# Hybrid retention / gated DeltaNet trunk: the DeltaNet steps' solve, spread and levels one slot later, with a new first step, start and end

## The reference

```python
h = rmsnorm(x, norm_g)
proj = h @ w_in                      # 1024 -> 9232: rq rk rv rz | dq dk dv dz | beta, a | two gates
o_r = retention(rope(rq), rope(rk), rv)        # 4 heads, dk 128, dv 256, chunks of 128
o_r = groupnorm(o_r) * silu(rz)
dq, dk, dv = silu(causal_conv(dq, dk, dv))     # 4 taps
o_d = gated_deltanet(l2norm(dq), l2norm(dk), dv, beta, g)   # 8 heads of 128
o_d = o_d * rsqrt(mean(o_d**2) + EPS) * dn_g * silu(dz)
y = sigmoid(gr) * (o_r @ w_up_r) + sigmoid(gd) * (o_d @ w_up_d)
x = x + y @ w_o
```

```python
v_new = u_n - w_n @ state
o = q_n @ state + attn_n @ v_new
state = state * exp(gl) + k_n.T @ v_new
```

## Time and profile before

| | us |
|---|---|
| median of 3 runs | 2670.03 (2669.53 to 2670.82) |
| the profiled execution | 2671.89 |
| its span | 2670.1 |
| TensorE busy in it | 2640.1 (99%) |
| VectorE busy | 1730.1 (65%) |
| ScalarE busy | 679.9 (25%) |
| GpSimd busy | 832.2 (31%) |
| mean granted TensorE clock | 0.998 |

### The profile page before, as it was taken

The page is one execution under the profiler, slowest core; times in us unless marked ns, Lnnn a source line. Parts: engine busy times, 40 slices in busy tenths (PEclk is TensorE's granted clock), DMA queues, the critical chain, the costliest instruction groups (busy, mean ns, idle before and its releaser), DMA issues.

```text
span 2670.1 us, 39962 instructions
## 1 busy us (share of the span) xinstructions
PE 2640.1 (99%) x14850; PEld 2255.1 (84%) x14850; DVE 1730.1 (65%) x3864; ACT 679.9 (25%) x1370; POOL 832.2 (31%) x459
## 2 busy tenths in 40 slices
PE   8999999999999999999999999999999999999998
PEld 6788888888898899888878888888888998888887
DVE  7878777877756555434587778777777555553333
ACT  5233333333312222200142232323332221231001
POOL 3233333333312112435432323232323122232443
PEclk9999999999999999999999999999999999999999
DMA  4331222222211112434532222222222111133344
GB/s 171 96 88 53 74 74 76 65 73 76 71 52 46 40 35 74 127 96 122 163 93 84 76 70 68 69 84 65 71 70 73 50 50 42 40 105 100 98 138 146
DMA packets 292980, 217.76 MB, mean 82 GB/s; under 512 B 31698, under 2 KB 246052, under 8 KB 292532
## 3 DMA queue, kind: packets, MB, share of 16 engines
q1 hardware_dynamic: 254884, 151.20, 19.8%
q10 hardware_dynamic: 37904, 64.01, 7.1%
HBM read 176.30 MB, written 38.86 MB: 81 GB/s over the span
## 4 chain that ended last, share of the span: by engine, by line
PE 89%; DVE 4%; DMA 3%; issue 1%; POOL 1%; SPq 1%; ACT 1%; ACTq 0%; DVEq 0%
PE dense_ps L819 22%; PE dense_ps L823 22%; PE dense_ps L821 22%; PE work L802 3%; PE dense_ps L843 2%; PE dense_ps L844 2%; PE dense_ps L845 2%; PE work L1077 1%; DMA arena<-l_scratch 1%; PE work L1114 1%; PE work L1053 1%; PE work L1036 1%; PE work L1134 1%; PE work L1103 1%; PE work L1127 1%
## 5 line engine op out<-in xcount | busy, mean ns | idle before, releaser
L819 PE MATMUL dense_ps<-act_hi,w_hi 128*128 128x512 f32 x2560 | 1052.3, 411 | 2.5 <-DVE act_lo L1766 1.5
L823 PE MATMUL dense_ps<-act_hi,w_lo 128*128 128x512 f32 x2560 | 1002.8, 392 | 0.0
L821 PE MATMUL dense_ps<-act_lo,w_hi 128*128 128x512 f32 x2560 | 1000.5, 391 | 0.0
L2459 POOL TENSOR_TENSOR w_lo<-w_raw,w_hi 128x1024 fp32r<-128x1024 f32 x162 | 400.1, 2469 | 1014.8 <-ACT w_hi L1350 572.2
L823 PEld LDWEIGHTS dense_ps<-act_hi,w_lo 128*128 128x128 f32 x2560 | 480.7, 188 | 107.0
L819 PEld LDWEIGHTS dense_ps<-act_hi,w_hi 128*128 128x128 f32 x2560 | 482.9, 189 | 86.7 <-issue 3.0
L821 PEld LDWEIGHTS dense_ps<-act_lo,w_hi 128*128 128x128 f32 x2560 | 483.4, 189 | 79.6 <-issue 0.5
L1883 DVE SCALAR_TENSOR_TENSOR arena<-arena,cols 128x512 f32<-128x512 f32 x288 | 242.6, 842 | 5.1
L1350 ACT ACTIVATE w_hi<-w_raw 128x1024 fp32r<-128x1024 f32 x88 | 92.7, 1054 | 327.5 <-PE dense_ps L823 309.9
L1340 ACT ACTIVATE arena<-dense_ps 128x512 f32<-128x512 f32 x96 | 57.4, 598 | 264.6 <-PE dense_ps L823 264.6
L1897 DVE SCALAR_TENSOR_TENSOR arena<-arena 128x512 f32<-128x512 f32 x96 | 112.5, 1172 | 13.9 <-ACT arena L1356 13.9
(11 more groups left out here) (248 smaller groups left out, 4040.2 us busy)
## 6 DMA issues: line engine op xcount, KB each, us to landing
w_raw<-in_w_in SPq DMA_DIRECT2D x138, 512.0 KB, 3.9
gate_scratch<-arena ACTq DMA_DIRECT2D x64, 256.0 KB, 2.1
arena<-gate_scratch ACTq DMA_DIRECT2D x64, 256.0 KB, 2.8
arena<-l_scratch SPq DMA_DIRECT2D x62, 256.0 KB
w_raw<-in_w_out SPq DMA_DIRECT2D x18, 512.0 KB, 3.6
o_scratch<-arena ACTq DMA_DIRECT2D x32, 256.0 KB, 2.0
w_raw<-in_w_up_dn SPq DMA_DIRECT2D x16, 512.0 KB, 3.7
arena<-o_scratch ACTq DMA_DIRECT2D x32, 256.0 KB, 3.8
```

Of the source, the lines that this page charges most:

```text
L819: eng.matmul(dense_ps[:, to, :], w_hi[:, slot, k, :], hi[:, k, seg], start=(k == 0), stop=False)
L821: eng.matmul(dense_ps[:, to, :], w_hi[:, slot, k, :], lo[:, k, seg], start=False, stop=False)
L823: mm = eng.matmul(dense_ps[:, to, :], w_lo[:, slot, k, :], hi[:, k, seg], start=False, stop=(k == KT - 1))
L2459: eng.tensor_tensor(w_lo[:, slot, :, :], w_from[second][:, :, :], w_hi[:, slot, :, :].bitcast(F32), ALU.subtract)\
```

## The change

In the regular steps (`even`, `odd`, `even_last`) the solve begins at slot 4 instead of 3, the spread stands at slot 9 instead of 8, each level one slot later, and `vt` at 20; no tap is placed in slots 4 to 8 instead of 3 to 7, so that slot 3 takes one. The list of slot 9 already holds `ks` of chunk 3, and the spread comes behind it; `turn 0` and `level_v 0` come ahead of `xu` in slot 10. The splits of weights stay where they are.

The first step gets a list of its own: solve from slot 16, spread at 21, levels at 23 to 31, the masks on VectorE instead of GpSimd, splits of the high parts on ScalarE, low parts on VectorE as steps of their own (`low`), both halves of the `l_scratch` load on SyncE's queue. At the start, tile 6's transposes go ahead of the dense pieces, `norm_rows(0, 1)` comes one piece later, `norm_diag(0, 1)` behind the loop of norms, and the split of the first weight ahead of a silu. At the end the last output block is computed in two halves of 256 tokens (`last_pieces`), transposes and squares are regrouped accordingly, means and powers come earlier, and tiles 4 to 7 are stored in halves of 512 columns.

```diff
@@ unit_schedule, first step
-        at(6, "mask", 0)
-        at(8, "dec", 0)
+        at(8, "split", 1)
+        at(9, "mask", 0)
+        at(9, "dec", 0)
         at(10, "nl", 0)
+        at(10, "low", 1)
...
-        at(15, "qe")
-        at(16, "kq")
-        slots[15].insert(0, ("mask", 1))
-        at(19, "dec", 1)
-        solve, spread_at, vt = 17, 24, 34
+        at(17, "kq")
+        at(20, "split", 2)
+        at(21, "spread")
+        at(21, "turn", 0)
+        at(22, "low", 2)
+        at(23, "level_v", 0)
+        at(23, "mask", 1)
+        at(23, "qe")
+        at(25, "level_x", 0)
+        at(25, "kq_decay")
+        at(25, "mask_t", 1)
+        at(26, "turn", 1)
+        at(26, "level_v", 1)
...
+        solve, spread_at, vt = 16, 21, 33
@@ unit_schedule, regular steps
-        solve, spread_at, vt = 3, 8, 19
+        solve, spread_at, vt = 4, 9, 20
+    else:
+        solve, spread_at = 4, 9
     if kind != "odd_last":
         for k in range(BASE - 1):
             at(solve + k // 3, "solve", k)
-        at(spread_at, "spread")
-        for n in range(NLV):
-            if first or n:
+        for n in range(NLV if not first else 0):
+            if n == 0:
+                at(spread_at, "spread")
+            if n:
                 at(spread_at + 1 + 3 * n, "turn", n)
                 at(spread_at + 1 + 3 * n, "level_v", n)
                 at(spread_at + 3 + 3 * n, "level_x", n)
...
-            spread(0 if 3 <= n < 8 else 1 if n < 18 and n not in (12, 16) else 2)
+            spread(0 if solve <= n < spread_at else 1 if n < 18 and n not in (12, 16) else 2)
@@ SyncE, load of l_scratch
-                    for c in range(0, CPH if u else 2, 2):
+                    for c in range(0, CPH, 2):
@@ TensorE, start
             turn_in(CPH + 1)
+            turn_in(CPH + 2)
...
-                        if k == 0:
-                            turn_in(CPH + 2)
-                        if k == 2:
+                        if k == 1:
                             turn_in(CPH + 3)
...
-                        if k == CPH:
+                        if k == CPH + 1:
                             norm_rows(l, 1)
@@ VectorE, layer start
-                silu(l * DH, 0)
                 eng.wait_ge(dense_ok[0].sem, dense_ok[0].after(n + 1, 2))
                 split_w(n + BLK_FIRST, BLK_FIRST % 2, held=False)
+                silu(l * DH, 0)
@@ TensorE, the last output block, in halves of 256 tokens
+            def last_pieces():
+                g = n + BLK_OUT + NHALF * KT - 1
+                for part in range(2):
+                    to = 1 - part
+                    seg = slice(HALF + part * HALF // 2, HALF + (part + 1) * HALF // 2)
+                    dst = dense_ps[:, to, 0:HALF // 2]
...
@@ SyncE, stores
-            for i in range(CPH + 1):
+            for i in range(CPH):
                 eng.wait_ge(out_ok, 2 * i + 2)
                 store(i, slice(0, D_MODEL))
+            eng.wait_ge(out_ok, 9)
+            store(4, left)
+            eng.wait_ge(out_ok, 10)
+            store(4, right)
```

More of the change, by code:

```diff
@@ L228, in unit_schedule @@
                 break
-            if pieces % (2 * KT) == 0 and (pieces or kind not in ("first", "odd_last")):
+            if pieces % (2 * KT) == 0 and not first and (pieces or kind != "odd_last"):
                 step = ("split", pieces // (2 * KT))
[L231 to L234, removed]
+                waiting.insert(0, step)
                 if kind == "even_last" and step[1] == 2:
@@ L1246, in _ @@
                           ready=(lambda b, k: None if b else (ol_ok.sem, ol_ok.after(l, k + 1))) if j == 0 else None)
-                for i in range(NHALF * KT):
+                for i in range(NHALF * KT if more else NHALF * KT - 1):
                     b, j = i // KT, i % KT
@@ L1271, in _ @@
                         turn_out(3)
-            for i in range(CPH, NCH):
-                turn_late(i)
+            for part, k in last_pieces():
+                if part == 0 and k == 4:
+                    for tile in (4, 5):
+                        turn_next(tile)
+                if part and k == 3:
+                    for tile in (4, 5):
+                        turn_late(tile)
+                if part and k == 4:
+                    for c in range(4):
+                        mm = turn_chunk(7, 0, c)
+                    mm.then_inc(out_ps, 1)
+                    turn_next(6)
+            for tile in (6, 7):
+                turn_late(tile)
         @block.scalar
@@ L1472, in delta_unit @@
                                 ret_v(l * RH, gg, int(of[2]), half)
-                        elif what == "split" and kind in ("even", "odd"):
+                        elif what == "split" and (kind in ("even", "odd") or kind == "first" and step[1]):
                             idx = g0 + step[1] + 1
@@ L2104, in delta_unit @@
                                .then_inc(qe_s.sem, 1)
-                        elif what == "kq":
+                        elif what == ("kq_decay" if kind == "first" else "kq"):
                             eng.wait_ge(kq_ps.sem, kq_ps.after(tn, 1))
@@ L2419, in _ @@
                     eng.sem_inc(dense_free[i % 2].sem, 1)
-                    if i >= NHALF * KT - 2:
+                    if more and i >= NHALF * KT - 2:
                         eng.sem_inc(dense_ok[i % 2].sem, KT)
@@ L2432, in _ @@
                                 norm_lo(l + 1, 0, k - 1)
-                    if not more and i in (KT + 2, KT + 5):
-                        final_mean((i - KT - 2) // 3)
+                    if not more and i == KT + 2:
+                        final_mean(0)
                     if not more and i in (KT + 3, KT + 4):
@@ L2533, in delta_unit @@
                                 split_w(g + idx, idx % 2)
-                        elif what == "mask":
+                        elif what == "mask" and kind != "first":
                             w = tn + step[1]
@@ L2616, in _ @@
                         norm_lo(l + 1, 0, 2 * (i - KT - 3))
-                    if not more and i in (KT + 2, KT + 5):
-                        final_power((i - KT - 2) // 3)
+                    if not more and i in (KT + 2, KT + 4):
+                        final_power((i - KT - 2) // 2)
                 if more:
```

140 lines of the change are left out of this document (92 added, 48 removed).

## The result

| | before | after |
|---|---|---|
| median, us | 2670.43 (2669.53 to 2670.97, 4 runs) | 2717.55 (2715.15 to 2719.93, 4 runs) |
| profiled execution, its span | 2671.89, 2670.1 | 2718.55, 2716.7 |
| granted TensorE clock, mean | 0.998 | 0.998 |

The changed kernel is slower: the ratio is 1.0176, with a 95% interval of 1.016 to 1.0191, or 47.1 us by the medians. The forecast was 2709 us, 39 us slower, with a range of 2662 to 2735.

A forecast was written before the change was run, and what follows sets the result against it. TensorE was taken to bound the kernel. Spread hold +43.2 and even steps' turn +5.3, less 9.5 won (loads, first steps, start, end), gave +39.0 on 2670.0: 2709 us, range 2662 to 2735.

The forecast's parts named there:

- What bounds the kernel: Whole kernel: TensorE, busy 2640.1 of 2670.1 us, so any delay to it in a repeated step is paid in full.
- The spread under GpSimd's subtraction, +43.2: Regular steps: spread held until GpSimd's subtraction ends, `level_v0` 1.44 us late in each of 30 steps, +43.2 us.
- The even steps' turn, +5.3: Even steps: `level_x1` waits 0.38 us for the level 1 copy, now behind other VectorE work, 14 times, +5.3 us.
- The late loads of `l_scratch`, -2.4: Regular steps: late `l_scratch` loads no longer matter with the solve a slot later, -2.4 us.
- First steps, -3.9: First steps of the layers: 60% of 6.5 us of TensorE waits won, -3.9 us.
- Start -1.3, end -1.9: Start: transposes fill a wait and `norm_rows` comes later, -1.3 us; end: stores begin earlier, -1.9 us.
- B: Regular steps: the spread isn't held by GpSimd, only the other terms stay, 2666 us; chance 0.14.
- C: Regular steps: the solve's last instruction is caught by GpSimd too, `level_v0` waits 2.95 us, 2754 us; chance 0.10.
- D: Regular steps: spread and GpSimd share and slow each other, spread takes 1.38 us, 2679 us; chance 0.05.
- E: TensorE's clock falls with the new idle times, coming on top, inside the range's upper end; chance 0.03.

The follow-up runs named there:

- e3: Changed kernel, with GpSimd's subtraction for split 1 of the regular steps first waiting for the spread to be done: 2668.14 us.
- e6: Changed kernel, with the spread put at the head of slot 9, ahead of `uu` of `ks3`: 2716.69 us.
- e1: Changed kernel, with the regular steps' solve, spread and levels back at their old slots (3, 8, 19): 2663.89 us, ratio 0.997.
- e2: Kernel before, with only the regular steps' solve, spread and levels moved one slot later: 2727.38 us, ratio 1.0211.
- e4: Changed kernel, with GpSimd's subtraction made of four instructions of a quarter each, no wait added: 2669.16 us.
- e5: Changed kernel, with GpSimd's subtraction cut in two instructions, over 6 and 2 of the 8 k-blocks: 2699.36 us, ratio 1.0108.

## Why the prediction was right, point by point

- **What bounds the kernel.** TensorE, and a delay in a repeated step is paid in full: an odd step grew by 1.55 us, the 1.44 that `level_v0` comes late and 0.10 for the restart. The retention stages, which the change doesn't touch, moved by 0.0 and -0.1 us. What I had not seen is that a long wait can be paid more than in full, by the clock behind it.
- **The spread under GpSimd's subtraction, +43.2.** Right in mechanism and in size. Predicted 1.44 us late, measured 1.44 (302.48 against 301.04); predicted end 0.55 us behind GpSimd's end, measured 0.55. Shown by e3 to e6, which change GpSimd's instruction or the spread's place. Missing was the restart of the group from a standstill, 0.10 us, which is 3 us over 30 steps, and that the two last even steps are not like the others. There the weight cast and `z_silu` stand ahead of `uu` on VectorE, and GpSimd's subtraction waits for that cast (it starts 0.81 us behind `ks3`, at 766.56 against 765.75, where in the even step shown above it was 0.07), so that `level_v0` waits 2.0 instead of 1.3 us, another 1.5; and the clock falls behind these waits, some 3.4.
- **The even steps' turn, +5.3.** Right. The distance between spreads grew by 1.99 us from an even step to the odd one behind it (298.47 and 343.65 before; 300.12 and 347.29 after) and by 1.58 from the odd to the next even one (387.98 before, 393.19 after): 0.41 us for the even step's own part, where I had 0.38.
- **The late loads of `l_scratch`, -2.4.** Wrong in sign. In four of the five steps of the earlier trace rows the waits are gone, as told. But in the changed kernel the solve waits for a late load in three regular steps, 1.95 us at 755.77, 2.62 at 1447.46 and 2.44 at 2099.60 (the first and the last are last even steps), and behind it the state's update and `uu` are late: L1148 waits 1.7 and 0.6 us, L1159 1.5 in three. That is 3.8 us where before it was 2.4 and where I had forecast none. Why the load is late in these steps stays open.
- **First steps, -3.9.** Too small: -3.5 and -5.3 by the stages, -8.8 in the profiled execution. I had taken 60% of the waits as won; of the 6.5 us nearly all went (0.5 us at `level_v0` is left in the first of the two). Most of what is left is the stretch at half the clock that the profiled execution of before has from 1362.3 to 1365.7, inside this stage, with a wait of 0.4 us just ahead of it; the one of the changed kernel has neither. By the median of e1 the gains outside the regular steps are 7 us in all, so the stages of one execution may flatter them.
- **Start -1.3, end -1.9.** -2.0 and -2.2. The first store is issued 7.3 us before the end of the span (2709.41 of 2716.7), where it was 7.2, so the stores themselves take no less; what is won lies ahead of them.

The sum of the terms went wrong in two directions: gains 6 us larger than forecast outside the regular steps (13.1 against 3.9 + 1.3 + 1.9 = 7.1), losses 13.6 us larger within them (59.7 against 43.2 + 5.3 - 2.4 = 46.1). Of the latter 4.5 us are the restart and the longer waits of the two last even steps, some 3.4 the half clock behind these, and 3.8 the loads; 2 stay unassigned. By the medians of e1 and e2 the picture is simpler: the gains are 7.1 us, as forecast, and the regular steps cost 56.4 alone where I had 46.1. Either way the term that was too small is the regular steps'.

Of the rivals, B (not held), C (the solve caught) and D (shared) fall by the changed kernel's own rows: spreads of 2.31 us, and `solve` instructions that are nowhere longer than 0.27 us, the last of the even step from 299.35 to 299.52. C had 0.15 us of room, from the start of that instruction to GpSimd's at 299.50; e6 shows that a spread 0.03 us behind GpSimd is held in full, and no run shows what becomes of a `solve` instruction there. Its price was also set too low: held to the mask's end at 303.83 + 0.55 the spread would make `level_v0` 3.16 us late, not 2.95, which gives 2761 us rather than 2754.

E (the clock) came true in part, on top of the forecast's case as it was told. The 28 waits of 1.3 us in the other regular steps left the clock at 1.00, but behind both waits of 2.0 us it was 0.50. e6, with the same two waits, has the same two stretches; e3, e4 and e5, where these waits are 0.7 to 1.4 us, have none in the regular steps. It is no strict rule: e2 has none behind its two waits of 2.0 us, but one behind a wait of 2.6 at 1793.22, and the stretches at the start of layer 1, in the kernel before and in e2, have a wait of only 0.4 us just ahead of them. A mean clock of 0.998 before and after doesn't tell of this; the stretches have to be looked at one by one.

By the rule of the Trainium skill (page "SBUF — State Buffer", section "SBUF: two separate sides") a VectorE instruction with two SBUF inputs and a GpSimd one that reads SBUF exclude each other: whichever starts first has the shared ports for the whole instruction, and the other is blocked. These traces agree, in both directions: VectorE's spread 2.31 instead of 0.69 us, GpSimd's subtraction 2.83 instead of 2.38.

## What to carry to other kernels

Where VectorE and GpSimd both work from SBUF, look for what GpSimd starts in the slot into which a short VectorE instruction is moved, and who waits for the short one. One slot later the spread took 2.31 us where one slot earlier it took 0.69, though every duration in the profile of before looks innocent: that GpSimd has slack, and VectorE too, says nothing. If the move is wanted all the same, let the engine with slack give way: a wait on GpSimd, or its instruction cut in pieces, each took 48 to 49 us off the changed kernel; but here leaving the regular steps' order alone (e1) was better still.

## What the runs showed that I had not expected

- At the boundary between two GpSimd instructions that stand one behind the other, VectorE gets in, even though GpSimd has its next one ready (e5: the spread, held 1.77 us, ends inside GpSimd's second piece; e4: 0.68 us for the spread, 3.74 for the four quarters). Cutting one GpSimd instruction was thus as good here as a semaphore, where the first piece was short enough to be over when the spread came; with three quarters it was not (e5).
- A group of matmuls that starts after a wait takes 0.84 us to the next start instead of 0.74, at an unchanged clock, after waits of 0.7 us (e3) as after those of 1.3. It is small, and it counts once for each wait.
- A wait of 2 us can cost TensorE another 1.7 us behind it, by a stretch at half the clock, and a mean clock of 0.998 doesn't show it.
- The runs of e1 spread over 7 us (2659.6 to 2666.86) and those of e3 over 2 (2667.47 to 2669.45), with the same first steps and ends. I did not find out why. A stretch at half the clock is worth 1.7 us, and the profiled execution of e1 has one near the start, from 13.2 to 16.6, that of e3 none before its end; whether the other executions differ in this can't be seen from their times.
